# First block's attention: values held stationary in column halves, probabilities normalised on GpSimd

## What is computed

```python
s = jnp.concatenate([s_loc.reshape(s_loc.shape[:5] + (n_loc,)), s_ctx], axis=-1)
p = jax.nn.softmax(s, axis=-1).astype(v.dtype)
...
o = (jnp.einsum('bhrnqjw,brnjwhd->brnqhd', p_loc, v_band)
     + jnp.einsum('bhrnql,blhd->brnqhd', p_ctx, vcx))
...
x = x + g1 * (jnp.concatenate([y_conv, y_attn], axis=-1) @ w_out[l])
```

## Time and profile before

| | |
|---|---|
| time, median of 3 runs | 1713.62 us (1712.37 to 1715.26) |
| span of the profiled execution | 1711.1 us |
| TensorE busy | 1397.3 us, 82% of the span |
| DMA on the chain that ended last | 47% of the span |
| TensorE on that chain | 47% of the span |
| attention loop, first T to the end of the last X in it | 143.0 to 173.2 us |

### The profile page before, as it was taken

The page is one execution under the profiler, slowest core; times in us unless marked ns, Lnnn a source line. Parts: engine busy times, 40 slices in busy tenths (PEclk is TensorE's granted clock), DMA queues, the critical chain, the costliest instruction groups (busy, mean ns, idle before and its releaser), DMA issues.

```text
span 1711.1 us, 21197 instructions
## 1 busy us (share of the span) xinstructions
PE 1397.3 (82%) x8724; PEld 855.2 (50%) x8724; DVE 536.3 (31%) x899; ACT 389.7 (23%) x579; POOL 132.3 (8%) x108
## 2 busy tenths in 40 slices
PE   4999997676666667757766766898999999999999
PEld 2986542222122112212221221476899998989997
DVE  2785310000000000000000000058365557835554
ACT  3515200000000000000000000057443346843332
POOL 1430000000000000000000000004500000730000
PEclk8999988877878877787877787899999999999999
DMA  9777599999999999999999999992154544425552
GB/s 376 263 290 301 228 382 426 429 427 429 429 429 429 429 428 429 429 428 428 428 429 428 428 429 429 428 344 99 52 195 179 178 162 149 143 99 197 195 179 93
DMA packets 80325, 542.05 MB, mean 317 GB/s; under 512 B 6312, under 2 KB 9721, under 8 KB 52626
## 3 DMA queue, kind: packets, MB, share of 16 engines
q1 hardware_dynamic: 76912, 535.93, 76.8%
q0 software_dynamic: 1632, 5.03, 1.0%
q10 hardware_dynamic: 1730, 0.36, 0.1%
HBM read 540.22 MB, written 1.08 MB: 316 GB/s over the span
## 4 chain that ended last, share of the span: by engine, by line
PE 47%; DMA 47%; DVE 3%; ACT 1%; issue 1%; POOL 1%; SPq 0%; DVEq 0%; ACTq 0%; POOLq 0%
DMA ring<-in_w_down 22%; DMA ring<-in_w_up 21%; PE bank L1387 10%; PE bank L1389 10%; PE bank L1388 10%; PE bank L1754 4%; PE bank L1773 3%; PE bank L1640 2%; DMA ring<-in_a_w_in 2%; DMA ring<-in_w_mod 1%; DMA ring<-in_w_in 1%; PE bank L1423 1%; PE bank L1621 1%; PE bank L1561 1%; PE bank L1733 1%
## 5 line engine op out<-in xcount | busy, mean ns | idle before, releaser
L1754 PE MATMUL bank<-ring,low 128*32 128x512 f32 x2016 | 314.5, 769 | 152.1 <-DMA ring<-in_w_up 125.7
L1754 PEld LDWEIGHTS bank<-ring,low 128*32 128x32 f32 x2016 | 66.6, 130 | 381.0 <-DMA ring<-in_w_up 192.5
L1773 PE MATMUL bank<-ring,low 128*32 128x512 f32 x976 | 167.7, 822 | 93.7 <-DMA ring<-in_w_down 86.6
L1133 ACT ACTIVATE low<-bank 128x512 f32<-128x512 f32 x16 | 9.6, 597 | 844.8 <-PE bank L1754 844.8
L927 ACT ACTIVATE ring_parts<-ring 128x4096 fp32r<-128x4096 f32 (+3 forms) x46 | 151.9, 3301 | 205.8 <-DMA ring<-in_mlp_w_down 101.0
L2083 DVE TENSOR_TENSOR ring_parts<-ring,ring_parts 128x4096 fp32r<-128x4096 f32 (+2 forms) x35 | 148.5, 4244 | 141.0 <-ACT ring_parts L927 141.0
L1388 PE MATMUL bank<-feat_parts,ring_parts 128*128 128x256 f32 x640 | 181.6, 284 | 0.0
L1389 PE MATMUL bank<-feat_parts,ring_parts 128*128 128x256 f32 x640 | 181.6, 284 | 0.0
L1387 PE MATMUL bank<-feat_parts,ring_parts 128*128 128x256 f32 x608 | 173.4, 285 | 6.8 <-DVE feat_parts L2153 3.7
L2429 DVE TENSOR_TENSOR low<-low,bank 128x512 f32<-128x512 f32 x16 | 11.0, 688 | 462.4 <-PE bank L1754 462.4
L1773 PEld LDWEIGHTS bank<-ring,low 128*32 128x32 f32 x976 | 31.7, 131 | 210.2 <-DMA ring<-in_w_down 135.3
(11 more groups left out here) (407 smaller groups left out, 1979.9 us busy)
## 6 DMA issues: line engine op xcount, KB each, us to landing
ring<-in_w_gate SPq DMA_DIRECT2D x64, 2048.0 KB, 25.7
ring<-in_w_up SPq DMA_DIRECT2D x62, 2048.0 KB, 23.0
ring<-in_w_down SPq DMA_DIRECT2D x61, 2048.0 KB, 26.2
ring<-in_mlp_w_up SPq DMA_DIRECT2D x16, 2048.0 KB, 7.8
ring<-in_mlp_w_down SPq DMA_DIRECT2D x16, 2048.0 KB, 7.9
ring<-in_w_mod SPq DMA_DIRECT2D x11, 2048.0 KB, 15.5
ring<-in_w_in SPq DMA_DIRECT2D x3, 2048.0 KB, 13.3
ring<-in_a_w_in SPq DMA_DIRECT2D x3, 2048.0 KB, 16.1
```

Source lines behind the costliest of these rows:

```text
L1754: last = pe.matmul((GATE if i < 4 else UP)[32 * j:32 * j + 32, :], xsT[:, k, :], held(n, 2)[:, kk, 512 * j:512 * j + 512], start=(k == 0), ...
L1773: last = pe.matmul(TURN[32 * g:32 * g + 32, :], hidT[:, c, 32 * j:32 * j + 32], down_row(n, c, d), start=(j == 0 and c < 2), stop=(j == 3 ...
```

## The change

It edits five places.

1. **O(j)** has its operands exchanged: a 128x64 block of `v1` is stationary and a 128x128 block of `pT` moves. The output is 64 partitions for each head, head 0 on partitions 0 to 63 and head 1 on 64 to 127 of one bank, so the result stands by feature at once. The loop over blocks is the outer one, the heads alternate inside. Banks alternate between 6 and 7 from j = 2 on.
2. **X(j)** and its copy on ScalarE are gone, `na_tok` too. VectorE's output(j) is now one copy of O(j) into `mixT` with the queries' order mirrored.
3. **share(j)** is new on VectorE: the reciprocal of the sums of step j, issued as soon as exps(j) are done. It stands ahead of max(j + 1) in VectorE's list.
4. **scale(j)** is new on GpSimd: two `tensor_scalar` instructions, each multiplying one head's 128x512 probabilities by its reciprocal in place.
5. **T(j)** waits for scale(j), head by head, where it waited for exps(j).

```diff
-            group(f"naO{j}", among=[6])
-        group("modT2", among=[7])
-        for j in range(N_NA):
-            group(f"naX{j}", among=[7])
+            group(f"naO{j}", among=[7 if j > 1 and j % 2 else 6])
+            if j == 0:
+                group("modT2", among=[7])
...
+            for j in range(N_NA):
+                pool.wait_ge(sem("na_share"), j + 1)
+                for h in range(2):
+                    p = na_p[2 * (j % 2) + h]
+                    pool.tensor_scalar(p, p, at_r[:, j % 4, h:h + 1], None, ALU.mult).then_inc(sem("na_scaled"), 1)
...
                     for h in range(2):
                         pe.wait_ge(*drained(f"naT{j}{h}"))
-                        n = HD * (2 * c + h)
-                        for b in range(4):
-                            last = pe.matmul(bk(f"naO{j}")[:, HD * h:HD * (h + 1)], pT[2 * (j % 2) + h][:, b, :], v1[:, b, n:n + HD],
-                                             start=(b == 0), stop=(b == 3))
+                    for b in range(4):
+                        for h in range(2):
+                            n = HD * (2 * c + h)
+                            last = pe.matmul(bk(f"naO{j}")[HD * h:HD * (h + 1), 0:P], v1[:, b, n:n + HD], pT[2 * (j % 2) + h][:, b, :],
+                                             start=(b == 0), stop=(b == 3), skip_group_check=True)
...
-                            pe.wait_ge(*drained(f"naS{j}{h}"))
+                            pe.wait_ge(sem("na_scaled"), 2 * j + h + 1)
...
-                    if j >= 2:
-                        local_turn(j - 2)
...
+                def share(j):
+                    for h in range(2):
+                        dve.wait_ge(*drained(f"naS{j}{h}"))
+                    dve.reciprocal(at_r[:, j % 4, :], at_s[:, j % 4, :]).then_inc(sem("na_share"), 1)
+
                 def output(j):
                     t, c = na_pair(j)
-                    for h in range(2):
-                        dve.wait_ge(*drained(f"naS{j}{h}"))
-                    link(dve.reciprocal(at_r[:, j % 4, :], at_s[:, j % 4, :]))
                     dve.wait_ge(*banks.filled(f"naO{j}"))
-                    dve.tensor_tensor(split(na_tok[:, t, P * c:P * (c + 1)], 2), split(bk(f"naO{j}")[:, 0:P], 2),
-                                      at_r[:, j % 4, :].unsqueeze(2).to_broadcast([P, 2, HD]), ALU.mult)\
+                    dve.tensor_copy(mixT[:, 4 + c, t * P:(t + 1) * P][:, ::-1], bk(f"naO{j}")[:, 0:P])\
...
                 for j in range(2):
                     for h in range(2):
                         maximum(j, h)
+                share(0)
                 for j in range(N_NA + 1):
                     between(j)
+                    if j + 1 < N_NA:
+                        share(j + 1)
```

More of the change, by code:

```diff
@@ L264, in two_blocks @@
         na_p = [pexp[0], pexp[2], xnf[:, 1024:1536], pexp[1]]
-        na_tok = cut(low, 0, NT, 512)
         SPAN = (T // GRID_W - 1) * RPB_C + GRID_W
@@ L1009, in exps @@
                                        accum_out=at_s[:, j % 4, h:h + 1]).then_inc(banks.drain_sem(f"naS{j}{h}"), 1)
[L1011 to L1015, removed]
                 exps(0)
@@ L1025, in attend_local @@
                                        ACT.Copy).then_inc(banks.drain_sem(f"naT{j}{h}"), 1)
-                    if j >= 2:
-                        output(j - 2)
-                output(N_NA - 2)
                 for i in range(2):
@@ L1034, in attend_local @@
                     last.then_inc(banks.drain_sem(f"yT{i}"), 1)
-                output(N_NA - 1)
             def attend_pairs(pre, parts_out, between=None, scale=None, beside=None):
@@ L1544, in mod_broadcast @@
                               start=True, stop=True), f"bc{i}")
[L1546 to L1550, removed]
             def attend_local():
@@ L1645, in _ @@
             heads, taps = (4, 5, 6, 7), (0, 1, 2, 3)
-            pe.wait_ge(*drained("naX3"))
+            pe.wait_ge(*drained("naO3"))
             need(wo1[0])
             mix_out(0, 0, heads, True)
-            local_turn(N_NA - 1)
             need(wo1[1])
@@ L1664, in _ @@
                 mix_out(1, n, taps, True)
-            pe.wait_ge(*drained(f"naX{N_NA - 1}"))
+            pe.wait_ge(*drained(f"naO{N_NA - 1}"))
             for n in range(2):
```

## The result

The changed kernel took 1717.65 us (median of 9 executions, 1716.14 to 1720.41), the one before 1713.64 (9 executions, 1712.37 to 1715.75). The two medians differ by 4.0 us; the ratio estimated from all the executions is 1.0027, 4.6 us, with a 95% interval of 1.0018 to 1.0037. The forecast was 1710.2 and the range ended at 1714.2.

What follows compares the result with a forecast made beforehand. TensorE was taken to bound the attention, DMA the experts. The turn 3.4 us earlier plus X's 0.1 gave a 3.5 us gain, from 1711.1 to a span of 1707.6, with 2.5 to the median 1710.2; range 1708.4 to 1714.2.

Steps and rivals of the forecast that it cites:

- What bounds it, and that the attention's time is passed on whole: Whole kernel: TensorE bounds the attention, DMA the experts' long stretch; time saved in the attention starts everything behind it earlier.
- share(0) to turn: Attention, first reciprocal's start to first transpose of the convolution's result; forecast 142.86 to 169.84, 26.98 us.
- TensorE's part: TensorE's work per attention step: T 0.97, S 1.06, new O 0.97, X gone; 3.00 us, against 3.98 before.
- GpSimd's multiply: New instruction scaling one head's 128x512 probabilities; its duration p taken as 0.70 us, ends 0.525 and 1.27.
- the two-step loop: Attention, through GpSimd's multiplies, T, S(j + 2), maxima and exponentials: 5.09 + 2p for two steps, binding above p = 0.73.
- the one-step loop: Attention, through share, the next maxima and exponentials on VectorE and ScalarE: 3.27 us per step, binding at the forecast p.
- The loops: Step on which attention loop binds after the change: 3.27 us per step, or 5.09 + 2p for two above p = 0.73.
- The sum: Attention's timeline: share(2) at 149.35, share(7) at 165.70, convolution's turn 3.4 earlier; with X's 0.1 a gain of 3.5 us.
- the turn: Convolution's start on TensorE after the attention, at 173.21 before; forecast 169.84.
- the last but one rival: TensorE's clock falls inside the attention, 3.0 us per fall: 1713.1 with one, 1716.1 with two; chance 0.07.
- the multiply is long: Rival: GpSimd's multiply takes 1.045 to 1.27 us and the loop over two steps binds, 1712.8 to 1714.6; chance 0.15.
- Slower by over 3.4 us: Whole kernel's time: outcome given 0.04, needing several falls of the clock or a wait not seen.

Runs made afterwards that it cites:

- e13: Changed kernel with two-operation multiply on GpSimd, S(j + 2) ahead of T(j), share(j + 1) between the heads of max(j + 2); 1706.86 us, against 1713.58 before.
- e11: Changed kernel with `tensor_tensor` multiply, S(j + 2) ahead of T(j), share(j + 1) between the heads of max(j + 2); 1708.38 us, against 1712.95 before.
- e2: Changed kernel with GpSimd's multiply as `tensor_tensor` with a broadcast reciprocal; 1712.74 us, against 1712.79 before.
- e10: Changed kernel with filler matmuls keeping TensorE busy during its waits for the first two multiplies; 1718.45 us, against 1713.58 before.
- e3: Changed kernel with GpSimd's 16 multiplies replaced by different forms and widths, most of the division left out; 1711.58 us in one execution, against 1712.95 before.
- e4: Changed kernel without GpSimd's multiplies, transposes waiting for the reciprocal, division left out; 1708.96 us, against 1712.79 before.
- e5: Changed kernel with S(j + 2) ahead of T(j) in TensorE's list, multiply unchanged; 1711.34 us, against 1712.79 before.
- e6: Changed kernel with S(j + 2) ahead of T(j) and GpSimd's multiply as `tensor_tensor`; 1708.60 us, against 1712.95 before.
- e7: Changed kernel with the multiplies moved from GpSimd to VectorE, right behind the reciprocal; 1714.12 us, against 1712.95 before.
- e12: Changed kernel with the second operation of GpSimd's `tensor_scalar` filled (plus 0); 1709.74 us, against 1713.58 before.
- e1: Changed kernel with GpSimd multiplying by a constant instead of the number per partition, division left out; 1717.93 us, against 1712.79 before.

## Why the prediction was wrong, step by step

- **What bounds it, and that the attention's time is passed on whole: right.** The attention grew by 4.65 us in the profiled execution, the span by 4.6, and over all versions the median followed "share(0) to turn" to within 1.6 us, from -6.2 (median -6.7) in e13 to +4.65 (+4.0) in the changed kernel.
- **TensorE's part: right.** O took 1.02 to 1.03, for 0.97. TensorE alone is 3.11 per step (e11), for 3.00. The change of form was taken a little too cheap: T ahead of the new O lasted 1.02 from start to start (e13), and 0.87 ahead of the old O of its own form, up to 0.15 for the 0.10. X went.
- **GpSimd's multiply: this step failed.** "nearest to the cast, with arithmetic added: I take p = 0.70, and keep 0.525 and 1.27 as the ends". The form as written takes 1.56, so the bounds from other operations didn't bound it, and with it the two-step loop, not the one-step loop of the forecast, set the pace. The nearest row was well chosen for another instruction than the one in the diff: with its second operation filled it takes 0.69. The operation that the diff leaves `None` was not in any row. By the figure of the Trainium skill's "GPSIMD Engine Reference", 3.1, which the prediction gave, 512 elements are 769 ns at best; the measured 1.56 and 0.69 lie on both sides of it.
- **The loops: right.** For two steps 5.09 + 2p gave 8.21, 7.17 and 6.47 at the measured p of 1.56, 1.04 and 0.69; the runs had 8.31, 7.22 and 6.56. The one-step loop is 3.20, for 3.27, so the two-step loop takes over a little earlier than the 0.73 of the prediction: at 0.69 it still binds.
- **The sum: right but for p.** At p = 1.56 it gives share(2) at 151.07, two pairs of steps and one step later share(7) at 170.76 and the turn at 176.6, with X's 0.1 a loss of 3.3 us. Measured were 4.0, interval of the ratio 3.1 to 6.3. At p = 1.04 it gave an attention 0.7 shorter than before, and e2's is 0.67 shorter; the time there could not be told from that of before.
- **The clock: it fell in the profiled execution, as the last but one rival had it, and cost about 1 us there, not that rival's 3.0.** The 3.0 doesn't follow from the rival's own step of 5.8 for 3.27 either, which is 2.5. Share(0) was 0.62 late, and share(2) came at 152.75, not 151.69: 1.06 more, of which S(2) alone is 0.95, and e10 without the fall was 0.95 shorter there. Taken off the 35.00, that leaves 34.05, where the sum gives 33.76 (142.86 to 176.62). In e2, e3, e4, e5, e6, e7, e11, e12 and e13 no fall lies inside the attention, in e1 there are two. A loss of 3.3 without any fall is inside the interval, so the median doesn't need it; whether the missing 0.7 is the clock is open.
- **The chances.** The rival "the multiply is long" was the right mechanism, with a chance of 0.15, and stopped at 1.27, as the range did. "Slower by over 3.4 us" had 0.04 and was tied to several falls of the clock or a wait not seen; it came, by a longer multiply in the loop that the prediction had written down.

## What to carry to other kernels

An instruction that no row shows is not bounded by its neighbours, least of all in a form that differs by an argument left empty: measure it by itself, or let the range go past the dearest row. Then ask in how many loops it stands. Here 2p stood twice in the ends and once in every pair of steps because S(j + 2) waited behind T(j) for no reason of its own; moving it (e5) brought the kernel from 4.0 us above the one before to 1.5 below it, with the instruction still slow. And GpSimd with the slower instruction (0.69), beside the other engines' work, beat VectorE with the faster one (0.48), where it lengthens the loop of every step.

## What the runs showed of the hardware

- GpSimd's `tensor_scalar` on 128x512 fp32, in place: one operation 1.49 to 1.50 with a constant, 1.56 with a number per partition; two operations 0.61 with constants, 0.69 with the number per partition and a constant. A copy 0.60; the broadcast `tensor_tensor` 1.04, and 0.61 on 256 columns.
- VectorE's one-operation form takes 0.48 (0.40 apart) on the same tile, the shortest of all forms that ran; two operations weren't tried there.
- TensorE with 64 columns stationary and 128x128 moving: 16 records of two heads in 1.02 to 1.03 us from their start to that of the next product, against 1.84 for the same products with 64 columns moving.
- TensorE's clock fell to its lower level (1.2 GHz, granted 0.50) for 3.4 us at a time inside the attention at different places: 147.5 in the changed kernel, 148.2 and 165.3 in e1, 173.9 in e10. In these three TensorE waited 8.4, 7.5 and 5.8 us for GpSimd, and in e3, without a fall, 5.5; but in e7 it waited 6.3 us for VectorE and the clock held. With one profiled execution of each, what brings a fall on is not shown.
